# Chunked linear attention: gated output y stored over v, q and k; the next tokens' h prepared inside the output tiles

## The reference

```python
h = rmsnorm(x, norm_g) * (1 + scale) + shift
proj = h @ w_in                       # q, k (512 columns each), v (1024), g_lr (16), r (1024)
log_a = log_sigmoid(g_lr @ w_alpha + b_alpha) / 16
...                                   # chunks of 64 tokens, 4 heads: o from q, k, v, decays
y = rmsnorm(o, gla_norm_g) * silu(r)
x1 = x + gate * (y @ w_out)
h1 = rmsnorm(x1, final_g)             # input of the second layer
```

## Time and profile before

| | |
|---|---|
| median of 3 runs | 2732.51 us (2730.07 to 2736.68) |
| span of the profiled execution | 2724.0 us |
| own time of the profiled execution | not given apart from its span |
| PE busy | 2500.2 us (92% of the span) |
| DVE, ACT, POOL busy | 1704.2, 1011.3, 763.2 us |
| linear attention layer (first four blocks) | about 60 to 1062.5 us of the span |
| projections begin | 1071.9 us |

### The profile page before, as it was taken

One profiled execution on the slowest core, in us unless ns is written; L12 is line 12 of the kernel. 1 busy time (PEld: TensorE's weight loads), 2 busy tenths in 40 slices (PEclk: granted clock), 3 DMA queues, 4 the chain that ended last, 5 costly groups with the idle time before them and its releaser, 6 DMA issues. The chain is left out here.

```text
span 2724.0 us, 34527 instructions
## 1 busy us (share of the span) xinstructions
PE 2500.2 (92%) x11297; PEld 1720.7 (63%) x11297; DVE 1704.2 (63%) x2698; ACT 1011.3 (37%) x1766; POOL 763.2 (28%) x353
## 2 busy tenths in 40 slices
PE   4998899999999997999999985999999999987998
PEld 1676677777777776777777762455554455546776
DVE  3236544553556361779897984777777777775664
ACT  4144453344435331322222123555445454452232
POOL 0233311101111100112101014666667666640000
PEclk8999999999999999999999995999999999998999
DMA  7964977478468647578666644111121111104334
GB/s 272 339 209 139 301 250 268 142 251 325 147 232 280 244 156 238 184 245 333 210 231 225 224 152 107 45 29 29 29 59 55 26 29 29 29 24 160 127 131 154
DMA packets 224426, 453.40 MB, mean 166 GB/s; under 512 B 23269, under 2 KB 81883, under 8 KB 224052
## 3 DMA queue, kind: packets, MB, share of 16 engines
q1 hardware_dynamic: 193256, 351.00, 38.3%
q10 hardware_dynamic: 31052, 100.87, 10.9%
HBM read 328.82 MB, written 109.35 MB: 161 GB/s over the span
## 5 line engine op out<-in xcount | busy, mean ns | idle before, releaser
L2086 DVE TENSOR_REDUCE att_mx<-att_bank_m 128x1 f32<-128x512 f32 (+1 forms) x640 | 365.1, 629 | 125.7 <-PE att_bank_m L1895 125.7
L554 PE MATMUL gla_bank_g<-mid_a_hi,mid_w_hi 128*128 128x512 f32 x1024 | 419.0, 409 | 23.7 <-DVE mid_a_lo L1072 10.4
L2035 ACT ACTIVATE att_p_f<-att_bank_s 128x512 f32<-128x512 f32 x576 | 316.9, 597 | 304.1 <-PE att_bank_s L1936 292.5
L554 PE MATMUL gla_bank_g<-mid_a_lo,mid_w_hi 128*128 128x512 f32 x1024 | 405.1, 396 | 0.0
L554 PE MATMUL gla_bank_g<-mid_a_hi,mid_w_lo 128*128 128x512 f32 x1024 | 405.0, 395 | 0.0
L1876 POOL TENSOR_TENSOR att_den<-att_den,att_p_f 128x1024 f32<-128x1024 f32 x160 | 379.7, 2373 | 59.4 <-ACT att_p_f L2035 48.5
L1601 DVE SCALAR_TENSOR_TENSOR proj_conv_acc<-proj_conv_in,proj_conv_w,proj_conv_acc 128x512 f32<-128x512 f32 (+1 forms) x480 | 357.8, 813 | 0.0
L1910 PE MATMUL att_bank_o<-att_p_f,att_v 128*64 128x512 f32 x1152 | 270.6, 605 | 0.0
L554 PEld LDWEIGHTS gla_bank_g<-mid_a_hi,mid_w_hi 128*128 128x128 f32 x1024 | 196.2, 192 | 87.9 <-issue 29.5
L554 PEld LDWEIGHTS gla_bank_g<-mid_a_hi,mid_w_lo 128*128 128x128 f32 x1024 | 195.8, 191 | 42.9
L554 PEld LDWEIGHTS gla_bank_g<-mid_a_lo,mid_w_hi 128*128 128x128 f32 x1024 | 196.7, 192 | 41.0 <-issue 2.4
(11 more groups left out here) (397 smaller groups left out, 4488.3 us busy)
## 6 DMA issues: line engine op xcount, KB each, us to landing
mid_w_hi<-scratch_w_hi SPq DMA_DIRECT2D x100, 512.0 KB, 4.3
mid_w_lo<-scratch_w_lo SPq DMA_DIRECT2D x100, 512.0 KB, 5.7
mid_w_hi<-scratch_w_hi ACTq DMA_DIRECT2D x84, 512.0 KB, 3.9
mid_w_lo<-scratch_w_lo ACTq DMA_DIRECT2D x84, 512.0 KB, 4.9
scratch_w_hi<-mid_w_hi SPq DMA_DIRECT2D x54, 512.0 KB, 6.3
scratch_w_lo<-mid_w_lo SPq DMA_DIRECT2D x54, 512.0 KB, 7.1
mod_wslab<-in_ada_w SPq DMA_DIRECT2D x6, 2048.0 KB, 18.5
first_w_raw<-in_gla_w_in SPq DMA_DIRECT2D x24, 512.0 KB, 6.0
```

What stands on the lines that cost most here:

```text
L554: last = pe.matmul(banks[s % 2][:], w[:, k, :], a[:, k, :], start=(k == 0 and n == 0), stop=(k == KT - 1 and n == 2))
L2035: act.activation(p_f[:, kt, :], S[kt % SBANKS][:], ACT.Exp, scale=float(HD) ** -0.5).then_inc(p_done, 1)
L2086: dve.reduce_max(mx[:, qt, n:n + 1], M[p % MBANKS][:, 0:min(TB, KEYS - TB * n)], AX_X).then_inc(mx_read, 1)
```

## The change

y gets places of its own, `y_hi_at` and `y_lo_at`, which lie over `v_tok` and `qk` (v, q and k of the block, read for the last time by unit 3 of the attention). `a_hi` and `a_lo` are then free from tile 23 on. In detail:

- `gate_y` is done in parts: 384 tokens of chunks 0 to 5 after unit 3's norm statistics, those of chunk 6 before tile 23's read-out, the last 128 tokens of chunks 0 to 6 in two instructions. ACT rounds chunks 0 to 6 (`round_y`) ahead of its work on tile 23, DVE writes the rest of chunks 0 to 4 there.
- SP loads the next x's halves in its queue at output tiles 0 and 1 instead of 1 and 2. ACT squares it at tiles 2 and 3, PE sums at tile 4 ahead of chunk 7, ACT takes the root at tile 4. `round_h` and `split_h` stand at tiles 5 and 6.
- In the last block `load_early_u` stands at tile 24.

```diff
+        with ExitStack() as same_places:
+            y_hi_at, y_lo_at = (same_places.enter_context(nc.sbuf_tensor(f"gla_{n}", [P, KT, TB], F32R)) for n in ("y_hi", "y_lo"))
+        v_tok = sb("v_tok", [P, NT, D])
         qk = sb("qk", [P, 2, GLA_H, TB])
...
-                            if c in (1, 2) and b + 1 < NB:
-                                half = slice(4 * (c - 1), 4 * c)
-                                sp.wait_ge(y_lo, UP + b * 8 + 4 * c)
+                            if c in (0, 1) and b + 1 < NB:
+                                half = slice(4 * c, 4 * c + 4)
+                                sp.wait_ge(y_lo, UP + b * 8 + 4 * c + 4)
...
+                        if j == 24 and b == NB - 1:
+                            sp.wait_ge(u_stored, UP + 32 * (NB - 1))
+                            load_early_u()
...
                 sp.wait_ge(proj, UP + NB * NW)
-                load_early_u()
                 load_early_pair(1)
...
-                        ahead = b + 1 < NB and c == 5
+                        ahead = b + 1 < NB and c == 4
                         gemm(b * 8 + 6 + c // 4, c % 4, first_wait=(y_lo, b * 8) if c == 0 else None,
-                             between=(lambda: sum_squares_of_x(b + 1)) if ahead else None)
+                             between=(lambda: sum_squares_of_x(b + 1)) if ahead else None, between_at=KT - 1, moving=(y_hi_at, y_lo_at))
...
                 def round_h(b, c):
                     act.wait_ge(x_scaled, UP + (b - 1) * 8 + c + 1)
-                    act.wait_ge(proj, UP + b * NW)
+                    act.wait_ge(proj, UP + (b - 1) * NW + NPROJ)
...
+                    def round_y(c):
+                        act.wait_ge(o_done, UP + (b + 1) * PER * GLA_H)
+                        act.wait_ge(y_part, UP + b * 7 + 7)
+                        act.wait_ge(y_done, UP + b * 3 + (3 if c == 7 else 1 + c % 2))
+                        act.activation(y_hi_at[:, c, :], xr[:, c, :], ACT.Copy).then_inc(y_hi, 1)
...
-                        if c in (3, 4) and b + 1 < NB:
-                            squares_of_x(b + 1, c - 3)
-                        if c == 5 and b + 1 < NB:
+                        if c in (2, 3) and b + 1 < NB:
+                            squares_of_x(b + 1, c - 2)
+                        if c == 4 and b + 1 < NB:
                             root_of_x(b + 1)
+                        if c in (5, 6) and b + 1 < NB:
+                            for k in range(4 * (c - 5), 4 * (c - 4)):
+                                round_h(b + 1, k)
                     if b + 1 < NB:
-                        for c in range(KT):
-                            round_h(b + 1, c)
                         square_x1(KT - 1)
```

More of the change, by code:

```diff
@@ L538, in _, with gemm @@
             def _(pe):
-                def gemm(group, s, banks=G, first_wait=None, between=None):
+                def gemm(group, s, first_wait=None, between=None, between_at=KT - 4, moving=(a_hi, a_lo)):
                     m = group * 4 + s
@@ L548, in gemm @@
                     for k in range(KT):
-                        if k == BETWEEN_AT and between is not None:
+                        if k == between_at and between is not None:
                             between()
@@ L552, in gemm @@
                             pe.wait_ge(first_wait[0], UP + first_wait[1] + k + 1)
-                        for n, (w, a) in enumerate(((hi, a_hi), (hi, a_lo), (lo, a_hi))):
-                            last = pe.matmul(banks[s % 2][:], w[:, k, :], a[:, k, :], start=(k == 0 and n == 0),
+                        for n, (w, a) in enumerate(((hi, moving[0]), (hi, moving[1]), (lo, moving[0]))):
+                            last = pe.matmul(G[s % 2][:], w[:, k, :], a[:, k, :], start=(k == 0 and n == 0),
                                              stop=(k == KT - 1 and n == 2))
@@ L919, in scale_x, with split_h @@
                         dve.scalar_tensor_tensor(xr[:, c, :], xr[:, c, :], gains[:, 0, c:c + 1], eb[:, 1, :], ALU.mult, ALU.mult).then_inc(x_scaled, 1)
-                def split_h(b):
-                    for c in range(KT):
+                def split_h(b, chunks):
+                    for c in chunks:
                         dve.wait_ge(h_hi, UP + b * 8 + c + 1)
```

56 lines of the change are left out of this document (32 added, 24 removed).

## The result

The changed kernel takes 2720.47 us (median of 6 runs, 2715.89 to 2725.78), the kernel before 2735.04 us on the same chip (6 runs, 2730.07 to 2746.14): a ratio of 0.9945, 95% interval 0.9927 to 0.9962, some 15 us less. The direction is the forecast's, the size is half of it, and the time lies above its range. The profiled execution of the changed kernel has a span of 2720.0 us.

A forecast was written before the change was run, and what follows sets the result against it. PE, busy 92% of the span, bounds the kernel; only its waits and lower-clock matmuls can go. Terms 1.4 + 9.1 + 6.6 + 0.5 + 3.9 + 7.5 = 29.0 us, off the median 2732.5, give 2703.5 us, range 2696 to 2716.

The forecast's parts named there:

- block 0: Block 0's stretch after tile 23: earlier start, but new waits for POOL's rests of weights; 337.7 against 339.07, gain 1.4 us.
- block 1: Stretch from tile 23's end to the next block's first matmul: shorter waits for y, squares and h; 46.35 us, gain 9.1.
- block 2: The same stretch in block 2, also forecast at 46.35 us: gain 6.6 us.
- block 3: Last block, no next x: 1.0 us gained, 0.5 taken off for u's loads ahead of tile 27's weight pair; gain 0.5.
- barrier: Way from the layer into the projections: SP's last DMA issue ends at 1063.4 instead of 1067.30; gain 3.9 us.
- projections to tile 20: Projections' start: earlier constants remove PE's waits of 4.46 and 0.47 us and 13 lower-clock matmuls; gain 7.5 us.
- the clock rival: Output tile 0's start: clock still falls behind waits of 1.75, 1.9 us in each of four blocks stay, 2711; chance 0.10.
- a tile of 24 matmuls takes 5.44 us: Time of every undisturbed output tile, used in all four stretches; eight tiles take 43.5 us.
- the waits listed: Block 0, PE waiting for POOL's rests of weights: 1.3 us at tile 4, 2.6 at tile 6, 3.9 at tile 7.
- one drop of 1.2: Block 0: one drop of the clock behind the weight waits, 1.2 us; the other only shortens the next wait.
- u behind the weights: Block 3's weight pair waits behind u: 4.25 us plus about 2 of lower clock, less 0.5; 2709; chance 0.08.
- The slower rival: SP's queue waits for y's rests ahead of weight pairs, two tiles per block wait, 6.9 us each; 2758; chance 0.04.

The follow-up runs named there:

- e4: Changed kernel with y's places moved to byte 99872, below x and the raw weights, instructions unchanged: 2715.05 us, ratio 0.9906 to the kernel before.
- e5: Changed kernel with 384 bytes of padding ahead of y's places: a y tile takes 5.45 us, against 5.58 in the changed kernel.
- e8: Changed kernel with 128 bytes of padding ahead of y's places: a y tile takes 5.45 us, against 5.58 in the changed kernel.
- e9: Changed kernel with 896 bytes of padding ahead of y's places: a y tile takes 5.45 us, against 5.58 in the changed kernel.
- e10: Changed kernel with y's places lower, u's loads spread, block 0's x loads one tile later and last two weight tiles rounded earlier: 2703.43 us, ratio 0.9861.
- e2: Changed kernel with the loads of u put back behind the layer's last output tile: 2726.55 us, ratio 0.9978 to the kernel before.
- e6: Changed kernel with u's four loads issued singly at steps 24, 26, 28 and 29 of block 3: 2716.03 us, ratio 0.9914 to the kernel before.

## Why the prediction was right in kind and wrong in size

The means of two traces of each kernel, in us:

| term | forecast | measured |
|---|---|---|
| block 0 | +1.4 | -6.8 (56.5 to 63.3) |
| block 1 | +9.1 | +6.7 (54.6 to 47.9) |
| block 2 | +6.6 | +7.0 (55.3 to 48.3) |
| block 3 | +0.5 | -4.4 (46.4 to 50.8) |
| barrier | +3.9 | +3.8 (9.5 to 5.7) |
| projections to tile 20 | +7.5 | +5.9 (143.1 to 137.2) |
| sum | 29.0 | 12.2; the runs say 15 |

**Barrier and projections: right.** SP's issues and the free queue gave what was forecast, and PE's wait for ctx went from 4.46 to 0.21. In the first trace of the changed kernel tile 20 came 7.4 us earlier, in the second 4.7.

**Blocks 1 and 2: right mechanism.** PE starts 1.73 and 1.93 behind tile 23 (forecast 1.75), at the full clock; no matmul at the lower clock follows the start, in this trace or in the 14 others of kernels with y's new places, so the clock rival fell, and PE never waits for h. The sum of squares waits 0.93 and 0.69 where 0.4 was taken. Without y's slow reads the stretches are 46.3 to 47.5 (traces of e4, e5, e8, e9 and e10), against 46.35. What failed is "a tile of 24 matmuls takes 5.44 us": true of h and of the old y, and I carried it over to places from which the trace had no tile's moving operand. It costs 0.13 a tile, 1.07 a block.

**Block 0: the step that failed is the list of what stands in a queue with the new work.** I costed ACT's and POOL's queues there, and SP's only as a rival for blocks 1 to 3. Of the waits listed, those of tile 6 and 7 came as 1.80 and 3.82 (forecast 2.6 and 3.9), tile 4's not at all. Not listed were tiles 2 and 3 (1.76 and 1.79, raw weights behind x) and tile 5 (0.50). The start took 3.51 instead of 2.1. Eight tiles, the sum of squares and all waits make 58.3; of the other 5 us, 3 are the lower clock (15 matmuls 0.43 apart instead of 0.23) and the rest slow restarts behind so many waits, where one drop of 1.2 was taken. Against the forecast's stretch of 55.1 the 63.25 are 8.2 more: 4.1 for the waits not listed, 1.4 for the start, 1.1 for y's slow reads and 3.8 for clock and restarts, less 2.2 for the listed waits, which came shorter. The start has a cause of its own, seen in DVE's three gated parts ahead of the rests of y in block 0 (behind an r read-out) and in block 1, and POOL's split in between:

```profile
279.94 0.68 DVE L1091 SCALAR_TENSOR_TENSOR first_xr<-gla_tmp,gla_bank_g 128x512 f32<-128x512 f32 x1
280.65 3.28 DVE L1048 SCALAR_TENSOR_TENSOR first_xr<-first_xr,half_gn,mid_x 128x384 f32<-128x384 f32 x3
...
533.67 1.81 DVE L1048 SCALAR_TENSOR_TENSOR first_xr<-first_xr,half_gn,mid_x 128x384 f32<-128x384 f32 x3
```

```profile
279.92 2.40 POOL L511 TENSOR_TENSOR mid_w_lo<-first_w_raw,mid_w_hi 128x1024 fp32r<-128x1024 f32 x1 [4.45 <-ACT mid_w_hi L727]
```

The three parts took 1.47 us more where POOL's split ran till 282.32: the first of them alone 2.08 instead of 0.62. The r read-out ahead of it, which reads one operand from a PSUM bank, took its usual 0.68 beside the same split. With the parts also begun 0.4 us later against tile 23's end, this makes up the start's 1.8 us over block 1's. POOL's nine splits there took 2.35 to 2.48, none of them 4.35 as in the earlier trace rows. *The Trainium skill, SBUF — State Buffer, Terms, has VectorE and GpSimd take the shared port pair for a whole instruction, so that the other "fully blocks"; the trace agrees, with DVE as the loser this time.* The forecast had drawn the loss on POOL's side only.

**Block 3: the rival "u behind the weights" was true**, with 3.48 us where it said 4.25, and 2.94 with the lower clock behind it in the second trace. I had the rate right (384 GB/s against 397). The bytes were 6.6 MB in my sum and some 7.6 when the wait ended, since tile 28's pair shared the engines. And I let them start at tile 23's end; the queue was drained then, and for the first 5.4 us the rate was 230 GB/s. e2 and e6 show that it was u, and that spreading it costs nothing. Of y's slow reads only the five tiles behind the wait add to the stretch (0.13 us each), since the pair sets the start of tile 27.

**The starting point** also misled: the first profiled execution of the kernel before was quick in block 2, and 8.5 us below the median. I took the difference off the median, which was sound. The size of block 2's gain rested on one draw of a wait that varies from 2.0 to 3.5 us, with its clock drop.

**The slower rival**, y's rests ahead of weight pairs in SP's queue, was false in blocks 1 to 3, where no such wait appears, and true in block 0, for raw weights. Its place was wrong, its mechanism was not.

What stays open: where the 3 us between the table's sum and the runs lie, why the kernel's other half varies by 12 us, what share each wait has in block 0's 5 us of lower clock and restarts, and what made its tile 7 wait 3.8 us in some traces and 2.3 in others.

## What to carry to other kernels

When work moves earlier, list every instruction that passes another in every queue, the loads of other operands above all. The stage in which those operands come raw is then a case of its own: here two guards for block 0, one in SP's order and one in ACT's, shortened its stretch by some 10 us (63.3 to 52.95, at most 1.0 of it by y's place). Spread a large prefetch between the loads with due times instead of issuing it in one piece. When a matmul operand gets a new place, measure its spacing from the trace, and try the same remainder by 256 bytes as its weights; here a pad of 128 bytes did it. What it is worth in time has to be timed: where another wait sets the end of a stretch, little of it shows.
